# Bias products in the first boundary's pauses, and the delta rule's heads split group by group before the output projection: a change to a one-core decoder kernel

## What is computed

```python
o = from_chunks(...)                                   # delta rule, 16 heads x 128
o = rms_norm(o, norm_w) * jax.nn.silu(z)
mix = o.reshape(B, L, 2048) @ w_out                    # the output projection, 2048 -> 1024
hs = hs + keep * rms_norm(mix, norm_w[i, 1])           # the first boundary
f = conv_ffn(rms_norm(hs, norm_w[i, 2]), ...)          # f0
hs = hs + keep * rms_norm(f, norm_w[i, 3])             # the second boundary
...
bias = rel_bias[rel_bucket(idx - qpos)]                # second block: 32 buckets x 8 heads
```

## Time and profile before

| | |
|---|---|
| median of 3 runs | 1655.83 us (1654.34 to 1656.16) |
| the profiled execution | 1656.0 us |
| its span, first to last instruction | 1654.1 us |
| mean granted clock of TensorE | 0.947 of 2.4 GHz |
| TensorE (PE) busy | 1591.9 us, 96% of the span |
| VectorE (DVE) busy | 1104.8 us, 67% |
| ScalarE (ACT) busy | 941.5 us, 57% |
| GpSimd (POOL) busy | 346.6 us, 21% |

### The profile page before, as it was taken

The page is one execution under the profiler, slowest core; times in us unless marked ns, Lnnn a source line. Parts: engine busy times, 40 slices in busy tenths (PEclk is TensorE's granted clock), DMA queues, the critical chain, the costliest instruction groups (busy, mean ns, idle before and its releaser), DMA issues.

```text
span 1654.1 us, 35020 instructions
## 1 busy us (share of the span) xinstructions
PE 1591.9 (96%) x14201; PEld 1494.9 (90%) x14201; DVE 1104.8 (67%) x2260; ACT 941.5 (57%) x1980; POOL 346.6 (21%) x409
## 2 busy tenths in 40 slices
PE   7998999998999999999999999999999999999998
PEld 6977987898889999897999999888999988899998
DVE  4775686566488865665689974766766566676664
ACT  6752664455256654445566764547676554567754
POOL 4231222233123322000313420201201210031010
PEclk9987896899799999899889999999999999999999
DMA  6320221134255555252336665544444655454452
GB/s 204 116 79 3 87 82 52 34 110 148 82 168 187 172 176 166 72 183 90 115 126 206 190 218 185 174 142 158 145 145 150 198 172 178 152 158 140 149 168 89
DMA packets 64977, 230.41 MB, mean 139 GB/s; under 512 B 7313, under 2 KB 9489, under 8 KB 64817
## 3 DMA queue, kind: packets, MB, share of 16 engines
q1 hardware_dynamic: 59792, 217.67, 41.2%
q0 software_dynamic: 4160, 8.98, 1.9%
q10 hardware_dynamic: 864, 1.52, 0.2%
HBM read 222.91 MB, written 5.24 MB: 138 GB/s over the span
## 4 chain that ended last, share of the span: by engine, by line
PE 76%; DVE 13%; ACT 5%; issue 4%; POOL 1%; DMA 1%; ACTq 0%; SPq 0%; DVEq 0%; POOLq 0%
PE ps L615 74%; DVE splitL L2259 4%; DVE arena L2267 3%; PE ps L619 2%; ACT splitH L1668 2%; ACT arena L1673 1%; DVE mixT L2264 1%; DVE arena L2264 1%; ACT sq L1673 1%; ACT L1673 1%; DVE arena L2275 1%; DMA ring<-wst 1%; POOL sq L3082 1%; ACT arenaR L1673 0%; DVE mixT L2267 0%
## 5 line engine op out<-in xcount | busy, mean ns | idle before, releaser
L2259 DVE TENSOR_TENSOR splitL<-ring,splitH 128x512 fp32r<-128x512 f32 x767 | 562.8, 763 | 245.9 <-ACT splitH L1668 237.2
L615 PE MATMUL ps<-aH,splitH 128*128 128x256 f32 (+2 forms) x2232 | 663.7, 298 | 14.5 <-DVE arena L2275 5.8
L615 PE MATMUL ps<-aH,splitL 128*128 128x256 f32 (+2 forms) x2232 | 643.0, 289 | 0.0
L615 PE MATMUL ps<-aL,splitH 128*128 128x256 f32 (+2 forms) x2232 | 628.0, 287 | 0.0
L1668 ACT ACTIVATE splitH<-ring 128x512 fp32r<-128x512 f32 x824 | 479.4, 623 | 134.4 <-PE ps L615 122.9
L615 PEld LDWEIGHTS ps<-aH,splitH 128*128 128x128 f32 x2232 | 432.3, 194 | 33.4 <-issue 15.8
L615 PEld LDWEIGHTS ps<-aH,splitL 128*128 128x128 f32 x2232 | 432.7, 194 | 0.0
L615 PEld LDWEIGHTS ps<-aL,splitH 128*128 128x128 f32 x2232 | 422.6, 192 | 0.4
L615 PE MATMUL ps<-arenaR,splitH 128*128 128x256 f32 (+2 forms) x1856 | 350.6, 289 | 8.6 <-DVE arenaR L2264 6.2
L615 PEld LDWEIGHTS ps<-arenaR,splitH 128*128 128x128 f32 x1856 | 292.9, 192 | 10.3 <-issue 6.4
L615 PE MATMUL ps<-arenaR,splitL 128*128 128x256 f32 (+2 forms) x928 | 265.3, 286 | 0.0
(11 more groups left out here) (207 smaller groups left out, 1272.0 us busy)
## 6 DMA issues: line engine op xcount, KB each, us to landing
ring<-wst SPq DMA_DIRECT2D x412, 512.0 KB, 3.8
mem_scratch<-arenaR POOLq DMA_DIRECT2D x16, 128.0 KB, 4.1
arenaR<-mem_scratch POOLq DMA_DIRECT2D x4, 512.0 KB, 8.6
rel_scratch<-arena POOLq DMA_DIRECT2D x8, 255.5 KB, 4.4
arena<-x SPq DMA_DIRECT2D x2, 512.0 KB, 4.9
arena<-mem POOLq DMA_DIRECT2D x2, 512.0 KB, 4.2
arena<-rel_scratch POOLq DMA_DIRECT2D x1, 1024.0 KB, 9.0
out<-arena ACTq DMA_DIRECT2D x4, 256.0 KB, 2.0
```

The lines of the kernel that those rows point to most:

```text
L615: return pe.matmul(out, lhsT, rhs, start=start, stop=stop)
L2259: dve.tensor_tensor(lo, raw, hi.bitcast(F32), ALU.subtract).then_inc(*inc(("lo_dve", q)))
```

## The change

1. The heads are cut group by group. `oH` and `oL` become four buffers of four heads each, in memory whose last reader is done earlier (`qkT`, `vTs`, the inverse's even-numbered buffers, for which the allocations are reordered). Group 0 is cut beside gate tile 9, group 1 beside tile 10, group 2 at the end of the stage, group 3 inside the projection. Group 3's low part moves from GpSimd to VectorE.
2. The projection's first three output tiles are computed in three rounds over the blocks: 0 to 7, 8 to 11, 12 to 15 (`OLD`). The first round of tile 0 stands ahead of the wait for the last `out` tasks. Its three banks are taken at once. Tiles 3 to 7 run as before, with two more banks borrowed.
3. The bias products are made of two fp32r matmuls of 512 columns in place of one fp32 one of 511; GpSimd makes the cut tables ahead of time (`tables`). The first three stand in TensorE's stream directly behind `nRb` of the first boundary, the other five in f0. ScalarE copies them out in place of VectorE, the first three ahead of its four `aH`.
4. At all three boundaries the reciprocal for `r2` stands ahead of `scale(0)` and `add(0)` in VectorE's stream.

```diff
-        oH, oL = al(16, T, r=True, at=16 * T), al(16, T, r=True, at=32 * T)
+        oH = [al(4, T, r=True, at=o) for o in (24 * T, 32 * T, even, 28 * T)]
+        oL = [al(4, T, r=True, at=o) for o in (even + 4 * T, even + 8 * T, even + 12 * T, 16 * T)]
+        OLD = (0, 8, 12, 16)
...
+            def biases(h):
+                b = bg.get("rel", h)
+                w.wait_ge("rcut")
+                mm(psum[b][:, :], relH[0:32, h:h + 1].broadcast_to([32, 128]), hotR[0:32, :], True, False)
+                mm(psum[b][:, :], relL[0:32, h:h + 1].broadcast_to([32, 128]), hotR[0:32, :], False, True).then_inc(*inc(("rel", h)))
+                bg.put(b, ("rrep", h))
...
+            def gdn_out():
+                bs = [fg.get("gdn", m) for m in range(3)]
+                for m, k in in_turn(16, OLD):
+                    if m >= 3:
+                        break
+                    if (m, k) == (1, 0):
+                        for c in range(3):
+                            yield from until("out", 3, c)
+                    h, l, end = take(128, ("gdn_w_out", 0, k * 128, 128 * m, 128))
+                    w.wait_ge("oL", k // 4)
...
             def rel():
-                yield 8.0
-                for h in range(8):
-                    b = bg.get("rel", h)
-                    w.wait_ge("rb")
-                    t = mm(psum[b][:, 0:511], relb[0:32, h:h + 1].broadcast_to([32, 128]), hot[0:32, :])
...
+                for h in range(RELS, 8):
+                    yield from room(bg, 1)
+                    biases(h)
+                    yield 0.6
...
+                def high(g):
+                    w.wait_ge("zg", g)
+                    w.wait_ge("zgp", g)
+                    w.wait_ge("vtr", 3, 2)
+                    w.wait_ge("qs", 2, 2)
+                    w.wait_ge("av", 2, 2)
+                    a(oH[g], oT[:, 4 * g:4 * g + 4, :], ACT.Copy).then_inc(*inc(("oH", g)))
...
+                w.wait_ge("ts2", i)
+                dve.reciprocal(tok("r2", n), tok("s2", n)).then_inc(*inc(("tr2", i)))
                 scale(0)
                 add(0)
-                w.wait_ge("ts2", i)
-                dve.reciprocal(tok("r2", n), tok("s2", n)).then_inc(*inc(("tr2", i)))
                 scale(1)
...
             def add_norm(mix, i, n):
...
+                if mix == "gdn":
+                    for h in range(RELS):
+                        biases(h)
                 highs(i, n)
```

More of the change, by code:

```diff
@@ L1190, in gdn @@
                         spawn(("core", ph))
-                for c in range(3):
-                    yield from until("out", 3, c)
+            def gdn_out():
[8 more added lines that the diff above has]
+                    w.wait_ge("oL", k // 4)
+                    t = mm3(psum[bs[m]][:, 0:T], h, l, (oH[k // 4][:, k % 4, :], oL[k // 4][:, k % 4, :]), k == 0, k == 15)
+                    signal(t, end, *([("tile", "gdn", m)] if k == 15 else []))
+                    if k == 15:
+                        fg.put(bs[m], ("nsc", "gdn", m))
+                    yield
+                borrow(2)
                 give_back()
+                yield from mix_sums("gdn", ("gdn_w_out", 0), 16, lambda k: (oH[k // 4][:, k % 4, :], oL[k // 4][:, k % 4, :]), T,
+                                    lambda k, part="lo": None, first=3)
+                repay()
             def ffn(name, layer, i, n, drop):
@@ L1720, in mix_sums @@
                 for m, k in in_turn(K, cuts):
+                    if name == "gdn" and (m, k) == (1, 0):
+                        for c in range(3):
+                            w.wait_ge("oT3", 3, c)
+                        a(oH[3], oT[:, 12:16, :], ACT.Copy).then_inc(*inc(("oH", 3)))
                     if cuts and (m, k) == (0, cuts[-2]):
@@ L2245, in rel @@
             def rel():
-                for _ in range(9):
+                for h in range(RELS, 8):
+                    biases(h)
                     yield
@@ L2662, in gdn @@
                                         late.append(gz)
+                                    if x in (9, 10):
+                                        low(x - 9)
                             yield
                     flush()
+                    if ph == 4:
+                        low(2)
                     yield
[L2666 to L2670 removed]
             def ffn(name, n, layer):
```

90 lines of the change are left out of this document (44 added, 46 removed).

## The result

| | before | after |
|---|---|---|
| median | 1655.09 us of 4 runs (1653.16 to 1656.16) | 1633.14 us of 4 (1629.28 to 1634.86) |
| ratio | | 0.9869, 95% interval [0.9849, 0.9888] |
| the profiled execution | 1656.0 us | 1634.17 us |
| its span | 1654.1 us | 1632.4 us |
| mean granted clock | 0.947 | 0.952 |

The change is faster by 22 us; 1638.0 was forecast, with 1633 to 1646 as the range. The time lies inside it, at its lower edge. So the first pair showed more than the change is usually worth. The question is where the 22 us came from.

A forecast was written before the change was run, and what follows sets the result against it. TensorE, 76% of the span, was taken as the bound, with its pauses and matmuls counted. Gains of 7.1 + 7.6 + 0.8 + 2.45 = 17.95 us took 1656.0 to 1638.0 us, range 1633 to 1646.

The forecast's parts named there:

- Part A, the pause: Projection's start: TensorE goes on right after gate tile 11's copy, 0.75 us lost instead of 6.36, gain 5.6 us.
- The rival that the pause comes back: Projection's first round: a late cut or oH ahead of weight splits stalls it; 1643 to 1645 us, chance 12%.
- Part A, the clock: Projection: the low-clock stretch behind TensorE's pause goes; 44% of 3.3 us of matmuls, 1.45 us, come back.
- The one from 427 to 437: Stretch where TensorE worked without a gap at granted clock 0.50; the prediction placed the norm's sums of tiny matmuls there.
- Part B: f0's bias products: eight fp32 ones cost 9.9 us, five fp32r pairs 2.3, gain 7.6 us (3.7 to 9.9).
- I take 2.3, since the columns and the mode are the same: f0: five pairs priced at 0.23 us a matmul, from fp32r rows of 512 columns with 128 rows.
- a sign of being wrong: Listed as showing the prediction wrong: steps above 0.3 us for the 512-column matmuls at full clock.
- its bounds: f0's bias products: the five new ones cost between nothing and 6.2 us, so the gain is 3.7 to 9.9 us.
- Part C: First boundary: earlier reciprocal and nRb, aH behind three bias copies, clock rising sooner; 0.8 us gained (-1.0 to 2.6).
- lets the clock rise sooner in f0: f0's start: TensorE without a pause from 446.8, so up to 1.8 us of low-clock time can come back.
- Part D: Second and third boundaries: normed(0) moves up by 1.2 and 1.25 us, 2.45 us in all (1.5 to 3).
- about 2 us either way: Whole kernel: allowance in the forecast's bounds for where the low-clock stretches fall.

The follow-up runs named there:

- the kernel without any change there: Kernel before with only the projection changed (heads split group by group, first round on heads 0 to 7): 1641.76 us against 1652.45, 0.9945.
- the two later pairs: The changed kernel against the kernel before, measured twice more on one and the same chip: 0.9904 and 0.9902, 16 and 17 us.
- the copies moved: Changed kernel with ScalarE's three first-boundary bias copies behind the aH copies of pairs 0, 1 and 2, not ahead: 1636.88 us, 0.9906 against before.

## Why the prediction was right, and where its sizes were off

- **Part A, the pause** (5.6): measured 5.55 in four profiles out of four. The prediction had the first matmul need groups 0 and 1; it needs group 0 alone, and what it waited for was the copy of tile 11, on which the forecast rested too. The rival that the pause comes back did not happen: TensorE has no idle time in the projection.
- **Part A, the clock** (1.45): 3.1. The step "so 44% of them, 1.45 us, come back" counted only the low stretch directly behind the pause. With the pause's stretch gone that step holds. The one from 427 to 437, which I had taken as given, also got shorter, by 3.4 us at the low level and so 1.5 of time, in each profile with the new start. But it was as short in the kernel with the bias part alone, which has the old start. So whether this second half of the 3.1 is the change's or scatter stays open. After the change it begins at 418.76, in the middle of TensorE's unbroken work and 10 us ahead of the norm's sums, so the place I had pointed to for it, the tiny matmuls of those sums, is not where the clock falls.
- **Part B** (7.6): 4.8 of length, 5.8 with the 2.3 us more of low clock in it counted out. The failed step is "I take 2.3, since the columns and the mode are the same": five pairs cost 5 x 0.85 = 4.3. The row I took it from had 128 rows, the products have 32, and the rows turned out to be what costs. The steps of 0.33 and 0.32 us around the second of the two matmuls were a sign of being wrong that the prediction names (above 0.3). With 8 x 1.25 before, B is 10.0 - 4.3 = 5.7, inside its bounds.
- **Part C** (0.8): 0.45, and not by its terms. `nRb` came 1.7 us sooner through the reciprocal, the three products with their copies cost 2.3, and the clock gave the remaining 1.05 (1.3 in the kernel without any change there). That it came out near 0.8 is luck. What I had called possible, that TensorE's unbroken work lets the clock rise sooner in f0, hardly came: the first 2.9 us of `aH` matmuls run at 0.50, before it were 4.0, so 0.5 us of the 1.8. Nor was the work unbroken: 1.32 us of idle time stood in front of `aH`. That `aH` cannot pass the copies, by the rule of the Trainium skill (page "TensorE: Matmul & The Clock Gate", Architectural detail) that the prediction cited, agrees with the trace: its input was ready at 436.6 and it began at 438.95, behind the third copy.
- **Part D** (2.45): 2.8 twice and 1.6 once. The difference lies in the second boundary, 8.0 us of it at the low level in that profile against 3.6 and 3.5 in the others.
- **The total.** 17.95 forecast; 15.4 to 16.8 in the pieces that the change touches. A was 1.6 too small and B 2.8 too large, which partly cancelled, so the good total says less for the terms than it seems. The 5 us up to the measured 22 are in pieces that the change was not to touch: 2.3 in the mLSTM stage, where the low stretches fell well this time, the rest in the idle time of the first piece and at the end. That the time came out 5 us below the forecast is chance, as the two later pairs show. I had allowed about 2 us either way for that; runs of one kernel differ by 7 us from their median.

## What to carry to other kernels

A price read from a row holds for that row's shape, rows included: between 128-row matmuls, one with 32 or 64 rows paid 0.39 us for the change, and zeros on the unused partitions removed it. Work put into a pause is hidden only if nothing that the pause waits for stands behind it on any engine: here the products filled TensorE's pause, but their copies stood ahead of the operand on ScalarE, and their matmuls outlasted the pause by 0.9 us, so the saving in f0 was spent at the boundary. And where the clock moves the total by 13 us, judge a part of 5 by the length of its own piece of the trace, low-clock time counted out, and by several profiles.

## What the runs showed that I had not expected

- The change between row counts costs 0.38 to 0.39 us, in fp32 (1.24 against 0.86) and fp32r (0.62 against 0.23), and only where 32-row or 64-row matmuls stand among 128-row ones. Six 32-row matmuls in a row behind the norm's follow each other at 0.43 us (2.90 us for the six, the last one's tail included), which is their 512 columns at 1.2 GHz. No such row of them ran at 2.4 GHz.
- The same kernel's stage of 989 or 990 matmuls took 139.9 us at clock 0.96 in one execution and 142.5 at 0.94 in another, with nothing different in its instructions. Such stretches lie otherwise from profile to profile: 8 to 11 us more of f0 fell to the low level with the copies moved, with the reciprocal alone or with the bias part alone, and took back 3.6, 3.6 and 4.7 us. Only for the bias part do the clocks of all its runs show that the kernel as a whole spent more time there. What sets their length I didn't find.
